# Second attention run in half steps between parts of the projections, on one Trainium2 core

## What is computed

```python
h = rms_norm(x, norm_mix)
q, k, v, u = split(h @ w_in, 4, axis=-1)                 # 512 columns each
# attention, 8 heads of 64 channels, causal, with ALiBi
s = q @ k.T * 64 ** -0.5 - slope[head] * (t - s_pos)     # causal mask
a = softmax(s) @ v
# pooling, 4 groups of 128 channels, windows w = 2, 4, 8, 16
mixed_g = (cs[t] - cs[t - w]) / min(t + 1, w) - u_g
p_g = (mixed_g @ w_pool[g]) * pool_scale
x = x + concat([a, p], axis=-1) @ w_out
x = x + square(relu(rms_norm(x) @ w_up)) @ w_down        # feed-forward, not touched
```

## Time and profile before

| | us |
|---|---|
| three runs | 1439.96, 1443.52, 1438.87; median 1439.96 |
| the profiled execution | 1438.98 |
| its span from the first to the last instruction | 1437.2 |
| PE busy in the span | 1321.6 (92%) |
| DVE, ACT, POOL busy | 635.2, 471.2, 247.1 |

### The profile page before, as it was taken

One profiled execution on the slowest core, in us unless ns is written; L12 is line 12 of the kernel. 1 busy time (PEld: TensorE's weight loads), 2 busy tenths in 40 slices (PEclk: granted clock), 3 DMA queues, 4 the chain that ended last, 5 costly groups with the idle time before them and its releaser, 6 DMA issues.

```text
span 1437.2 us, 25329 instructions
## 1 busy us (share of the span) xinstructions
PE 1321.6 (92%) x10577; PEld 1170.4 (81%) x10577; DVE 635.2 (44%) x763; ACT 471.2 (33%) x758; POOL 247.1 (17%) x228
## 2 busy tenths in 40 slices
PE   5788898988879999999999986988899999999998
PEld 5556577877779988998889985866898899988998
DVE  5425763545525644113443356445355442244323
ACT  4324433433425332222222241356442321122221
POOL 6000232523200221002221012101003210022100
PEclk9999889999989999999999998999899999999999
DMA  5212110000114322233232222200322222232321
GB/s 182 66 58 88 53 35 1 3 2 3 61 54 143 98 89 88 88 103 96 92 118 89 89 67 88 88 1 0 103 87 90 88 88 89 91 106 94 103 88 59
DMA packets 99927, 108.93 MB, mean 76 GB/s; under 512 B 1906, under 2 KB 97188, under 8 KB 99844
## 3 DMA queue, kind: packets, MB, share of 16 engines
q1 hardware_dynamic: 99764, 107.45, 23.2%
q0 software_dynamic: 80, 0.26, 0.1%
HBM read 105.60 MB, written 2.10 MB: 75 GB/s over the span
## 4 chain that ended last, share of the span: by engine, by line
PE 75%; DVE 9%; issue 5%; ACT 4%; DVEq 2%; POOL 2%; ACTq 1%; POOLq 0%; DMA 0%
PE ps L399 10%; PE ps L400 10%; PE ps L401 10%; PE ps L434 9%; PE ps L436 9%; PE ps L435 9%; DVE w_lo L1381 2%; PE ps L485 1%; PE ps L487 1%; PE ps L486 1%; PE ps L427 1%; PE ps L425 1%; PE ps L426 1%; DVE rcnt L1849 1%; PE ps L651 1%
## 5 line engine op out<-in xcount | busy, mean ns | idle before, releaser
L1381 DVE TENSOR_TENSOR w_lo<-w_raw,w_hi 128x2048 fp32r<-128x2048 f32 (+1 forms) x93 | 212.4, 2284 | 281.3 <-ACT w_hi L968 278.0
L434 PE MATMUL ps<-w_hi,a_hi 128*128 128x256 f32 x1024 | 288.1, 281 | 0.9 <-DVE w_lo L1381 0.9
L435 PE MATMUL ps<-w_lo,a_hi 128*128 128x256 f32 x1024 | 287.7, 281 | 0.0
L436 PE MATMUL ps<-w_hi,a_lo 128*128 128x256 f32 x1024 | 287.7, 281 | 0.0
L399 PE MATMUL ps<-h_hi,w_hi 128*128 128x512 f32 x672 | 272.8, 406 | 13.1 <-DVE w_lo L1381 12.6
L400 PE MATMUL ps<-h_lo,w_hi 128*128 128x512 f32 x672 | 268.7, 400 | 0.0
L401 PE MATMUL ps<-h_hi,w_lo 128*128 128x512 f32 x672 | 268.3, 399 | 0.0
L968 ACT ACTIVATE w_hi<-w_raw 128x2048 fp32r<-128x2048 f32 (+1 forms) x90 | 171.2, 1903 | 169.7 <-PE ps L436 141.1
L2079 POOL TENSOR_TENSOR hsq<-tmp 128x512 f32<-128x512 f32 x64 | 103.4, 1617 | 568.2 <-ACT tmp L972 568.2
L434 PEld LDWEIGHTS ps<-w_hi,a_hi 128*128 128x128 f32 x1024 | 192.9, 188 | 1.5 <-DVE w_lo L1381 1.3
L435 PEld LDWEIGHTS ps<-w_lo,a_hi 128*128 128x128 f32 x1024 | 193.0, 188 | 0.2
(11 more groups left out here) (317 smaller groups left out, 1851.7 us busy)
## 6 DMA issues: line engine op xcount, KB each, us to landing
w_raw<-w_ffn_up_dram SPq DMA_DIRECT2D x16, 1024.0 KB, 5.4
w_raw<-w_ffn_down_dram SPq DMA_DIRECT2D x16, 1024.0 KB, 5.2
w_raw<-w_up_dram SPq DMA_DIRECT2D x16, 1024.0 KB, 5.4
w_raw<-w_down_dram SPq DMA_DIRECT2D x16, 1024.0 KB, 5.1
w_raw<-w_in_first_dram SPq DMA_DIRECT2D x12, 1024.0 KB, 5.4
w_raw<-w_out_dram SPq DMA_DIRECT2D x8, 1024.0 KB, 6.3
w_raw<-w_in_dram SPq DMA_DIRECT2D x8, 1024.0 KB, 5.5
xn<-x_dram SPq DMA_DIRECT2D x8, 512.0 KB, 6.7
```

The costliest lines, as they stand in the source:

```text
L434: mm(o, hi[:, hb + k, tok], whi, start=first and own and k == ks[0], stop=False, skip_group_check=True)
L435: mm(o, hi[:, hb + k, tok], wlo, start=False, stop=False, skip_group_check=True)
L436: m = mm(o, lo[:, hb + k, tok], whi, start=False, stop=last and k == ks[-1], skip_group_check=True)
L1381: v.tensor_tensor(w_lo[:, g % 2, :, 0:n], w_raw[:, g % 2, :, 0:n], w_hi[:, g % 2, :, 0:n].bitcast(F32), ALU.subtract).then_inc(sm["w_lo_re ...
```

## The change

- The u groups stay. Then six groups follow in the order `IN2`: (q and k of pair 0), (v of pairs 0 and 1), (q and k of pair 1), (v of pairs 2 and 3), (q and k of pair 2), (q and k of pair 3). A group "qk" now holds 128 columns of q and 128 of k, loaded by two DMAs of 512 KB.
- Each of the last four of these groups, and the first two of the out projection, is cut into eighths (1/8 of its matmuls). After each eighth all three engines call `tick(n)`, n = 0 to 47. Pair p has its eight half steps from tick `PAIR_AT[p]` = 0, 8, 24, 32 on. Scores of both heads come at even ticks, weights are transposed two ticks after, and multiplied by v three ticks after.
- Scores use the two halves of the array straight from `qkT` (K = 64), so POOL's staging goes. The bias of each head is written once by POOL (eight instructions over 512 columns), and DVE uses one fused instruction for bias and minimum.
- The split of the next group's weights stands at the second eighth of each group, on ACT ahead of that tick's work and on DVE behind it.
- The out projection is cut by input halves: first all four row tiles and 512 output columns with the pooled half (`m_hi`, `m_lo`), then the same with the attention half, then the second 512 output columns likewise. The attention's output is turned at ticks 20, 22, 40 and 44 and split at ticks 33, 35, 40 and 44.
- Pooling: only the first 16 positions have counts of their own. `rcnt` is 4 by 16, positions from 16 on use the constant 1/w. The four windows stand ahead of the split of the third input group, the pooled tiles are split straight from PSUM.
- ACT and DVE take the sums of the first 512 columns of the out projection at its half: four adds of 512 columns, four `part` of 512 columns, and ACT's split of the last group behind these.

```diff
@@ load
-            with sp.Fori(0, 2) as i:
-                for c in range(2):
-                    load(G_QK2 + c, w2[:, bass.ds(i * 512 + c * GW, GW)], i, 2)
...
+            for n, (kind, p) in enumerate(IN2):
+                g = G_IN2 + n
+                if kind == "v":
+                    load(g, w2[:, 1024 + p * GW:1024 + (p + 1) * GW])
+                else:
+                    sp.wait_ge(sm["w_lo_ready"], g - 1)
+                    for k in range(2):
...
@@ tensor
+            def tick(n):
+
+                m = half_step(n)
+                if m is not None and m % 2 == 0:
+                    scores2(m)
+                m = half_step(n - 2)
+                if m is not None:
+                    turn_weights2(m)
+                m = half_step(n - 3)
+                if m is not None:
+                    values2(m)
+                if n in MIX_AT:
+                    turn_mix2(MIX_AT.index(n))
...
+                channels(0, None)
+                pe.wait_ge(sm["wpool_loaded"], 16)
+                pooled(0)
+                pooled(1)
+                tokens(1, None)
+                pooled(2)
+                pooled(3)
+                for n in range(2, 6):
+                    (channels if IN2[n][0] == "qk" else tokens)(n, 8 * (n - 2))
...
-            attention(1)
-            pe.wait_ge(sm["hlo_ready"], H_OUT2 + 8)
-            for c in range(2):
-                natural_group(G_OUT2 + c, T_OUT2 + 2 * c, 0, h_hi, h_lo)
-            out_pair(N_FFN2, G_OUT2 + 2, T_OUT2 + 4)
+            in_and_attention()
+            last_pair(N_FFN2, G_OUT2 + 2, T_OUT2 + 4, mixed_rows)
@@ scalar
+                for n in range(2, 6):
+                    for i in range(8):
+                        if i == 1:
+                            split(G_IN2 + n + 1)
+                        if i == 5:
+                            mixed(n, 0)
+                        tick(8 * (n - 2) + i)
+                    mixed(n, 1)
...
+            in_and_attention()
+            act.wait_ge(sm["tile_evacuated"], T_OUT2 + 4)
+            for c in range(TT):
+                part(xn[:, c, 0:2 * GW], c, 0)
             split(G_OUT2 + 3)
@@ vector
+            def biased2(m):
...
+                v.tensor_tensor_reduce(out=Z2[:, n % 2, e, 0:w], in0=bias[:, 2 * p + e, (TT - 1 - t) * P:S], in1=ps[:, 4 + e, 0:w],
+                                       scale=1.0, scalar=3.0e38, op0=ALU.add, op1=ALU.min, accum_out=negmax2[:, m:m + 1])\
+                    .then_inc(sm["max_ready"], 1)
...
+            for n in range(6):
+                for i in range(8):
+                    tick(8 * n + i)
+                    if i == 1:
+                        split(G_IN2 + n + 3)
+            for c in range(TT):
+                if c % 2 == 0:
+                    dve.wait_ge(sm["mm_done"], 2 * G_OUT2 + 2 + c // 2 + 1)
+                o = xn[:, c, 0:2 * GW]
+                v.tensor_tensor(o, o, ps[:, (T_OUT2 + c) % 4, :], ALU.add).then_inc(sm["tile_evacuated"], 1)
             split(G_OUT2 + 3)
@@ gpsimd
+            for h in range(H):
+                m = g_.tensor_scalar(bias[:, h, :], delta[:, :], float(2.0 ** (-8.0 * (h + 1) / H)), None, ALU.mult)
+            m.then_inc(sm["bias_built"], 1)
```

More of the change, by code:

```diff
@@ L257, in cols_of, with landed, half_step, wide @@
             return slice(g * GW, (g + 1) * GW)
+        def landed(g):
+            twice = (G_IN2 + n for n, (kind, p) in enumerate(IN2) if kind == "qk")
+            return 16 * (g // 2 + 1 + sum(t <= g and t % 2 == g % 2 for t in twice))
+        def half_step(tick):
+            for p, t in enumerate(PAIR_AT):
+                if t <= tick < t + 2 * TT:
+                    return 2 * TT * p + tick - t
+            return None
         def two(x):
             return x.rearrange("p (q n) -> p q n", q=2)
+        def wide(w, g):
+            return w[:, g % 2, :, :].rearrange("q (k a) n -> q k (a n)", a=2)
         def by_k(x):
@@ new lines, in pooled, with channels @@
+            def pooled(g):
+                pe.wait_ge(sm["window_ready"], g + 1)
+                if g >= 2:
+                    pe.wait_ge(sm["hlo_ready"], H_OUT2 + g - 1)
+                mm(ps[:, 6 + g % 2, :], wpool[:, g, :], uT[:, g, :], start=True, stop=True).then_inc(sm["pooled"], 1)
+            def channels(n, base):
+                g, tile = G_IN2 + n, T_IN2 + 2 * n
+                pe.wait_ge(sm["w_lo_ready"], g + 1)
+                for j in range(2):
+                    pe.wait_ge(sm["tile_evacuated"], tile + j - 3)
+                    o = ps[:, (tile + j) % 4, :]
+                    for k in range(KT):
+                        whi, wlo = (w[:, g % 2, k, j * P:(j + 1) * P] for w in (w_hi, w_lo))
+                        mm(o, whi, h_hi[:, k, :], start=k == 0, stop=False)
+                        mm(o, whi, h_lo[:, k, :], start=False, stop=False)
+                        m = mm(o, wlo, h_hi[:, k, :], start=False, stop=k == KT - 1)
+                        if k == KT - 1:
+                            m.then_inc(sm["mm_done"], 1)
+                        if base is not None and k % 2:
+                            tick(base + 4 * j + k // 2)
@@ new lines, in tokens @@
+            def tokens(n, base):
+                g, tile = G_IN2 + n, T_IN2 + 2 * n
+                pe.wait_ge(sm["w_lo_ready"], g + 1)
+                for c in range(TT):
+                    if c % 2 == 0:
+                        pe.wait_ge(sm["tile_evacuated"], tile + c // 2 - 3)
+                    for k in (0, 4):
+                        m = row_product(ps[:, (tile + c // 2) % 4, c % 2 * GW:(c % 2 + 1) * GW], rows(c), g, 0, h_hi, h_lo, k == 0, k == 4,
+                                        own=c % 2 == 0, ks=range(k, k + 4))
+                        if c % 2 and k:
+                            m.then_inc(sm["mm_done"], 1)
+                        if base is not None:
+                            tick(base + 2 * c + k // 4)
@@ new lines, in mixed_step, with mixed_rows @@
+            def mixed_step(o, c, g, hi, lo, k, first, last):
+                whi, wlo = wide(w_hi, g)[:, k, :], wide(w_lo, g)[:, k, :]
+                mm(o, hi[:, k, rows(c)], whi, start=first, stop=False)
+                mm(o, hi[:, k, rows(c)], wlo, start=False, stop=False)
+                return mm(o, lo[:, k, rows(c)], whi, start=False, stop=last)
+            def mixed_rows(c, late):
+                g = G_OUT2 + 2 + late
+                for k in range(HP):
+                    m = mixed_step(ps[:, (T_OUT2 + 4 + c) % 4, :], c, g, *((m_hi, m_lo), (h_hi, h_lo))[late], k,
+                                   late == 0 and k == 0, late == 1 and k == HP - 1)
+                return m
@@ L1117, in _, with qk @@
                 rkv_tiles(G_RKV + 2, T_RKV + 4, i)
-            def qk(g, tile, rwkv=False):
+            def qk(g, tile):
                 with act.Fori(0, 2) as i:
```

412 lines of the change are left out of this document (219 added, 193 removed).

## The result

The kernel after takes 1402.07 us (median of four runs, 1401.62 to 1403.15) against 1439.64 for the kernel before in the same session: a ratio of 0.9735, 95% interval 0.9716 to 0.9753. The change gives 37.6 us. I had forecast 1415 and a range from 1404: the direction is right, but the forecast gain was 24.7, and the time falls 2 us under the range.

The account below looks back on a forecast made before the run. PE was busy 92% of the span, so only its idle or slow stretches could give time. Terms 12.7 - 1.2 + 8.4 + 7.2 + 2.2 - 2.9 - 1.7 = 24.7 off 1439.0 gave 1414.3, stated as 1415, range 1404 to 1428.

Parts of the forecast that it names:

- 16 counts: Second block's pooling: the 12.95 us reciprocal shrinks to under 1 us, its stall and slow clock go; saves 12.7 us.
- Pooling: Pooling matmuls: four take 5.8 us for 4.6, with a 2.3 us wait ahead of the third; costs 1.2 us.
- Windows against POOL: Rival: DVE's pooling windows stand still for all 12.3 us of POOL's bias writing; +7.4 us, 1422; chance 0.05.
- The attention: Second block's attention: 42 us of PE work, 3 of returns, 4 of waits, 49.0 for 57.4; saves 8.4 us.
- Returns: In the ticks: PE coming back to the projection costs 0.08 us at some 36 ticks, 3 us in all.
- the turning: Transposing the attention's output: 2.0 us between other work instead of 9.2 before; saves 7.2 us.
- Out projection: First two quarters run without a wait ahead, at full clock: 22.4 us for 24.6; saves 2.2 us.
- The pair: Out projection's last pair: PE waits 3.3 us for 0.4 before, costs 2.9; slow clock behind it costs 1.7.
- Outside: Code the change does not touch, such as the feed-forward parts: the sum had no term for it.
- Waits in every group: Rival: splits not hidden by two ticks, PE waits in four groups with half steps; about +19 us, 1434; chance 0.13.
- The clock in the interleaved part: Rival: short matmuls with small gaps get half speed, +9.4 us a group, 1471 with all six; chance 0.04.
- Cheaper than counted: Rival: the waits found in the attention are absorbed and returns cost nothing; 1406; chance 0.12.

Follow-up runs that it names:

- e1: Kernel after plus an unused 64-byte-per-partition tensor where `slopes` stood, so later tensors lie at the addresses of before; 1410.37 us.
- e3: Kernel before with only the 16 counts per pooling group (new windows in the old order), tensors at the old addresses; 1425.42 us.
- e9: Kernel after with ACT's last out split ahead of the four sums and the first two pooled evacuations ahead of the v tile's; 1395.13 us.
- e4: Kernel after with ACT's split of the last out group ahead of the four sums instead of behind them; 1398.24 us.
- e2: Kernel before with `slopes` in a free part of the parameter tile, so later tensors lie 64 bytes lower, as in after; 1435.85 us.
- e8: Kernel after with all 48 ticks in one piece before the out projection, no eighths between, the out split moved ahead of the first tick; 1424.66 us.
- e6: Kernel after with 96 unused bytes per partition where `slopes` stood; one execution, 1384.31 us.
- e12: The kernel of e6 timed again in four runs; median 1392.77 us, 1382.26 to 1396.93.

## Why the prediction fell short

From the end of the first group of q and k, 871.51, to 1032.47 are 160.96 us; I had forecast 192.2 - 24.7 = 167.5. So 6.5 of the 12 or so missing us lie there, and 5.5 outside.

Two steps of the prediction failed, and it took both to leave the range: the attention, counted at 49.0 us, took 42.7, and all code outside the change, put at nothing without a reason, gave 5.5. With either one as forecast the profiled 1402.3 would have been 1407.8 or 1408.6. At the addresses of before, where the second falls away, e1 took 1410.4: inside the range, 29.7 gained for the 24.7 forecast.

| part | forecast | measured |
|---|---|---|
| v group and pooling, 871.5 to 888.5 | 17.2 | 17.0 |
| ticks with the pair's free pieces, to 1005.4 | 124.1 | 116.9 |
| to 1008.67, the wait in the pair | 3.3 | 3.3 |
| the rest of the pair, 21.2 before | 22.9 | 23.8 |

- *16 counts* (12.7): right within a microsecond; e3 shows 13.8 in its stretch. *Pooling* (-1.2, with a wait of 2.3): right, 2.1; e9 shows that it was a matter of order. *Windows against POOL*: DVE's split took 2.65 for 2.29 and a copy 0.83 for 0.43 while POOL wrote the bias, POOL's eight instructions took 14.2 us for the 12.3 counted, and DVE's chain ended at 881.9, a microsecond ahead of my 883. The rival did not come about. The Trainium skill, SBUF — State Buffer, "SBUF: two separate sides", would have had one of the two stand still for whole instructions of the other; the trace does not agree: between 859.9 and 871.5 DVE was busy for 10.0 and POOL for 11.2 of 11.6 us, and DVE's instructions grew by 0.4 at most.
- *The attention* (49.0) is the first step that failed. Of the 116.9 us six groups at 11.2 take 67.2 and the pair's pieces 5.6; 44.1 remain. Four times four transposes of the output take 1.4 (I took 2.0), so the attention has 42.7. Three terms differ. Scores are as counted (3.0 per pair). Transposes and products are cheaper: 2.3 and 3.8 for 2.7 and 4.8, or 5.4 in four pairs; the earlier trace rows was read in the first attention, where other rows stood around them: the eight matmuls take 0.81 here for 0.94 there. Within after itself three transposes take 0.38 to 0.39 behind scores, as I had taken it, and 0.32 to 0.33 behind the projection, four 0.49 and 0.44. Waits were 0.9 for 4.0; of the places that I named only tick 35's division showed one. Returns cost more: 42.7 - 4 x 9.15 - 0.9 = 5.2 for 3, some 0.13 at the 39 returns that the trace shows, the eighth of six matmuls taking 1.49 to 1.57 for 1.40. 5.4 + 3.1 - 2.2 = 6.3; with 0.6 of the turning and 0.3 of the four groups (44.8 for 45.1) that is the 7.2 of the table.
- *Out projection*: the quarters cost what was said. *The pair*: the wait was 3.1 for 3.3, forecast to its releaser. The clock behind it cost 2.6, not 1.7: it stayed at 1.2 GHz for 6.8 us, while the low stretch behind 833.90, at 3.4 us, is of the size that the 1.7 stands for. e4 shows wait and clock together at 6.1.
- *Outside*, the second step that failed: nothing was counted, and 5.5 us came. The prediction does not look at the removed `slopes` tensor at all. Moving the others by its 64 bytes was worth 4.3 us even in the kernel before (e2, 1440.11 - 1435.85), and the two feed-forward parts, at 2.1 and 2.3, give the same. The 1.1 left is the start of the execution, which varies as much by itself.
- *The rivals.* Waits in every group: none over 0.7. The clock in the interleaved part: 1.00 throughout. "Cheaper than counted" (0.12) came half true: the waits did vanish, but the returns cost more and not nothing, and what made up for it, cheaper transposes and products, stood in no rival. By its own terms (4.0 and 3) it should have said 1408, not 1406; that the time came out on its side owes as much to the addresses.

What remains open is why the pace of the feed-forward matmuls depends on the place of tensors, and why with 96 bytes executions differ; no run here tells it. That transposes and products are cheaper because of what stands around them is read from the traces, not tested by a run.

## What to carry to other kernels

When a chain of short dependent steps (scores, exponential, transposes, product) waits for itself, lay its pieces between the pieces of an independent product: here the same operations took 44.1 us with cover and 65.2 without, of which 5 to 10 are owed to where e8 put a split. Then price the pieces by PE's own start-to-start times in like surroundings, and count few waits where the cover between two steps is longer than the chain: here two ticks between each step and the next, 2.4 to 2.6 us apiece, left 0.9 us of wait in all. In in-order engines ask of each item which later one is waited for: moving one split ahead of four sums took away 3.1 us of wait and the slow clock behind it. And when a change adds or drops a tensor, compare it at equal addresses before crediting it.

## What the runs showed of the hardware

- Moving tensors by 64 bytes per partition changes the time of untouched matmuls: a stretch of 369.84 us took 367.70, and 360.14 with 96 bytes more than after. In the down projection 768 matmuls of 256 columns in a row take, from the first start to the last, 90.76 us in before (559.27 to 650.03, 0.1183 each), 89.49 in after (0.1167) and 86.95 in e6 (0.1134), all at a granted clock of 1.00. With the 96 bytes two paces occur: e12 has 86.95 us in its first block and 90.34 in its second. Over the placements of the table the whole time went from 1384 to 1411.
- Waits of 3.1 to 3.5 us do not always lower the clock: behind the 3.13 in after it was at 1.2 GHz for 6.8 us, behind the same wait in e8 it stayed at 2.4. Nor is a shorter wait safe: behind the wait of 2.27 for `h_lo` at the second feed-forward part the next 6 us had 1.00 in after and e4, but 0.72 in e8 and e9, and that part took 1.5 us longer there. The rows of after around the wait (us, PE busy, clock, DMA share, GB/s):

```profile
1007.70:1009.40 1.70, 0.73 (x2) 0.55 0.00 0
1009.40:1014.80 5.40, 5.40 (x15) 0.51 0.61 194
```

- PE busy for 116 of 116.9 us with pieces of 128x64, 128x128, 64x512 and 128x512 in turn kept the full clock.
